# A two-layer hybrid backbone on one core: the third mixer's level scores with one product per level for both directions

## What is computed

```
def step(S, blk):
    qc, kc, vc, gc = blk
    b = jnp.cumsum(gc, axis=2)
    diff = b[:, :, :, None, :] - b[:, :, None, :, :]
    pair_decay = jnp.where(causal[:, :, None], jnp.exp(jnp.minimum(diff, 0.0)), 0.0)
    att = jnp.einsum('bhtd,bhsd,bhtsd->bhts', qc, kc, pair_decay)
    o = jnp.einsum('bhtd,bhdv->bhtv', qc * jnp.exp(b), S) + jnp.einsum('bhts,bhsv->bhtv', att, vc)
```

## Time and profile before

| | us |
|---|---|
| median of 3 runs | 1773.2 (1769.05 to 1775.02) |
| the profiled execution | 1773.12 |
| its span | 1771.1 |
| TensorE / weight load busy | 1602.1 / 1270.0 |
| VectorE / ScalarE / GpSimd busy | 1088.9 / 638.6 / 75.5 |
| mean DMA rate over the span | 103 GB/s, 182.01 MB |

### The profile page before, as it was taken

How to read it: one execution, slowest core, us unless ns; L and a number is a source line. 1 busy time by engine, 2 the same in 40 slices (tenths; PEclk the granted TensorE clock), 3 DMA queues, 4 the chain that set the end, 5 groups by cost and what they waited for, 6 DMA issues and landing times. The chain is left out here.

```text
span 1771.1 us, 29499 instructions
## 1 busy us (share of the span) xinstructions
PE 1602.1 (90%) x12128; PEld 1270.0 (72%) x12128; DVE 1088.9 (61%) x1868; ACT 638.6 (36%) x1062; POOL 75.5 (4%) x112
## 2 busy tenths in 40 slices
PE   6999999789789999999999979999968699889996
PEld 4766776655578778888887757678755587768875
DVE  2286347887866674554443354735788767668765
ACT  4254222433431254222222252433244321356651
POOL 0000011300101000000000000000020100000000
PEclk8999999989999999999999989989989899989999
DMA  9311111167201134222232022212234101345550
GB/s 391 140 48 49 55 53 60 57 242 260 76 3 50 41 127 167 95 95 95 96 118 72 1 87 83 73 48 83 73 118 146 50 2 50 119 191 186 181 204 24
DMA packets 41620, 182.01 MB, mean 103 GB/s; under 512 B 4752, under 2 KB 5520, under 8 KB 33680
## 3 DMA queue, kind: packets, MB, share of 16 engines
q1 hardware_dynamic: 41488, 180.14, 28.5%
HBM read 179.08 MB, written 1.05 MB: 102 GB/s over the span
## 5 line engine op out<-in xcount | busy, mean ns | idle before, releaser
L235 PE MATMUL ps<-hr_in,wr_in 128*128 128x512 f32 (+1 forms) x544 | 222.0, 408 | 14.2 <-DVE wr_in L228 13.1
L236 PE MATMUL ps<-hr_in,wr_in 128*128 128x512 f32 (+1 forms) x544 | 209.0, 384 | 0.0
L237 PE MATMUL ps<-hr_in,wr_in 128*128 128x512 f32 (+1 forms) x544 | 208.4, 383 | 0.0
L235 PEld LDWEIGHTS ps<-hr_in,wr_in 128*128 128x128 f32 x544 | 108.4, 199 | 63.7 <-issue 35.4
L228 DVE TENSOR_TENSOR wr_in<-mix,wr_in 128x1024 fp32r<-128x1024 f32 x68 | 83.9, 1235 | 95.5 <-ACT wr_in L224 91.5
L235 PE MATMUL ps<-mix_r,work_r 128*128 128x512 f32 (+1 forms) x352 | 133.8, 380 | 1.6 <-DVE work_r L228 1.6
L236 PE MATMUL ps<-work_r 128*128 128x512 f32 (+1 forms) x356 | 135.1, 379 | 0.0
L228 DVE TENSOR_TENSOR work_r<-pr,work_r 128x2048 fp32r<-128x2048 f32 x38 | 87.0, 2288 | 71.2 <-ACT work_r L224 67.0
L237 PE MATMUL ps<-mix_r,work_r 128*128 128x512 f32 x320 | 124.5, 389 | 0.0
L2970 PE MATMUL ps<-mix_r,work_r 128*128 128x512 f32 x336 | 121.4, 405 | 2.3 <-DVE mix_r L228 2.3
L237 PEld LDWEIGHTS ps<-hr_in,wr_in 128*128 128x128 f32 x544 | 108.2, 199 | 19.7
(11 more groups left out here) (522 smaller groups left out, 3314.2 us busy)
## 6 DMA issues: line engine op xcount, KB each, us to landing
mix<-in_w_in SPq DMA_DIRECT2D x68, 512.0 KB, 3.5
pr<-in_w_up SPq DMA_DIRECT2D x28, 1024.0 KB, 4.9
pr<-in_ada_w SPq DMA_DIRECT2D x40, 512.0 KB, 6.3
ring<-in_w_up SPq DMA_DIRECT2D x16, 1024.0 KB, 4.9
ring<-in_ada_w SPq DMA_DIRECT2D x28, 512.0 KB, 4.3
pr<-in_w_down SPq DMA_DIRECT2D x14, 1024.0 KB, 4.8
pr<-in_ada_w SPq DMA_DIRECT2D x8, 1024.0 KB, 15.7
work<-in_w_out SPq DMA_DIRECT2D x16, 512.0 KB, 3.6
```

The source lines that it names most:

```text
L235: nc.tensor.matmul(out, sh, mh, start=first, stop=False)
L236: nc.tensor.matmul(out, sh, ml, start=False, stop=False)
L237: return nc.tensor.matmul(out, sl, mh, start=False, stop=last)
```

## The change

Level scores of both directions come from one product. Of a block, the first half holds keys scaled for the forward direction and queries scaled for the backward one, the second half the reverse; the product's two off-diagonal quadrants are the forward and the backward scores. `steps` becomes (None, 0, 6, 1, 2, 3, 4, 5), eight entries. Step None is the diagonal: the keys of both directions are added, the queries taken unscaled, and collecting multiplies by the identity, which also writes the zeros that the GpSimd clear made before. The other levels are collected by a masked copy over all 128 columns into one image `at` of half the size. The widest level (number 2 of the steps, `WHOLE`) has no differences on VectorE: ScalarE makes its exponentials straight from the cumulated decay with a bias per partition, 64 columns at a time, and copies its quadrants out of PSUM itself (`collect_whole`). The keys' end decay is likewise made by ScalarE with a bias, 128 columns at a time. The read-out takes one image, so it has half the products. The extra work moves to other step numbers, and the jobs are dealt out over steps 1 to 7, so `late` holds five numbers in layer 0 and two in layer 1.

```diff
     vT = take(1024)
-    at = take(4096)
+    at = take(2048)
+    expo = (A1, take(2048))
     st = take(1024)
     A0 = take(3072)
-    expo = (A0[:, 0:1024], A1[:, 0:1024])
-    keys = (A0[:, 2048:3072], A1[:, 1024:2048])
+    keys = (A0[:, 0:1024], A0[:, 2048:3072])
...
-    steps = [(d, l) for l in range(LEVELS) for d in range(2)]
+    ecol, middle = tiles(mix, 0, 1)[:, 16:32], tiles(mix, 0, 1)[:, 32:48]
+    steps = (None, 0, LEVELS - 1, *range(1, LEVELS - 1))
+    WHOLE = 2
 
...
-    TURN_AT, PRODUCTS_AT, JOBS_AT = (3, 5), 7, 1
-    UNIT_AT = (11, 12)
-    KEYS_EXP_AT, QUERIES_EXP_AT, ENDS_EXP_AT, KEYS_OUT_AT = (1, 2), (4, 6), 3, (5, 7)
+    KEYS_AT, STATES_AT, QUERIES_AT = (2, 3), 6, (4, 5)
+    TURN_AT, PRODUCTS_AT, JOBS_AT = (3, 4), 5, 0
+    UNIT_AT = (6, 7)
+    KEYS_EXP_AT, QUERIES_EXP_AT, ENDS_EXP_AT, KEYS_OUT_AT = (1, 2), (3, 4), 3, (4, 5)
     use = len(steps) * len(pairs)
     ready = len(pairs) * (STATES_AT + 1)
...
                         pe.wait_ge(S("kv_out"), 1)
                     for b in range(4):
                         t0 = (b % 2) * T + jj[b // 2] * P
                         for q in range(2):
-                            mm = nc.tensor.matmul(score_bank(n, m, q)[:, b * P:(b + 1) * P], keys[d][q * HD:(q + 1) * HD, t0:t0 + P],
-                                                  queries[d][q * HD:(q + 1) * HD, t0:t0 + P], start=True, stop=True)
+                            mm = nc.tensor.matmul(score_bank(n, m, q)[:, b * P:(b + 1) * P], keys[n % 2][q * HD:(q + 1) * HD, t0:t0 + P],
+                                                  moving[q * HD:(q + 1) * HD, t0:t0 + P], start=True, stop=True)
                     mm.then_inc(S("s_mm"), 1)
                 if n in TURN_AT:
...
-                    for d in range(2):
-                        for q in range(2):
-                            hd = 2 * i + q
-                            mm = nc.tensor.matmul(ps[4 + i][q * HD:(q + 1) * HD, j * P:(j + 1) * P], vT[:, j * 256 + hd * HD:j * 256 + (hd + 1) * HD],
-                                                  at[:, d * 2048 + (4 * j + hd) * P:d * 2048 + (4 * j + hd + 1) * P],
-                                                  start=j == js[0] and d == 0, stop=False)
+                    for q in range(2):
+                        hd = 2 * i + q
+                        mm = nc.tensor.matmul(ps[4 + i][q * HD:(q + 1) * HD, j * P:(j + 1) * P], vT[:, j * 256 + hd * HD:j * 256 + (hd + 1) * HD],
+                                              at[:, (4 * j + hd) * P:(4 * j + hd + 1) * P], start=j == js[0], stop=False)
                 for j in js:
...
 
             pe.wait_ge(S("low_rank"), 1)
-            pe.wait_ge(S("at"), 2 * (idle_from + 1))
+            wait_collected(pe, idle_from)
             lora(0, 0)
             for p in late[:-2]:
...
@@ -1774,39 +1779,52 @@
 
             def exponents(n):
 
-                d, l = steps[n]
-                cv, dv = blocks(tiles(cum, 2 * d, 2), l), blocks(expo[d], l)
-                ref = (1 << l) - 1 if d == 0 else 1 << l
-                if n >= 2:
-                    dve.wait_ge(S("kf"), n - 1)
-                nc.vector.tensor_tensor(dv, cv, cv[:, :, :, ref:ref + 1].to_broadcast(list(cv.shape)),
-                                        ALU.subtract).then_inc(S("dv"), 1)
+                l = steps[n]
+                for d in range(2):
+                    cv, dv = blocks(tiles(cum, 2 * d, 2), l), blocks(tiles(expo[n % 2], 2 * d, 2), l)
+                    ref = (1 << l) - 1 if d == 0 else 1 << l
+                    if n == WHOLE:
+                        ins = nc.vector.tensor_scalar(middle_of(d).rearrange("p i (b t) -> p i b t", t=1), cv[:, :, :, ref:ref + 1], -1.0, None, ALU.mult)
+                    elif l == 0:
+                        ins = nc.vector.tensor_tensor(dv[:, :, :, 1 - d:2 - d], cv[:, :, :, 1 - d:2 - d], cv[:, :, :, d:d + 1], ALU.subtract)
+                    else:
+                        ins = nc.vector.tensor_tensor(dv, cv, cv[:, :, :, ref:ref + 1].to_broadcast(list(cv.shape)), ALU.subtract)
+                ins.then_inc(S("dv"), 1)
 
             def factors(n):
-                d, l = steps[n]
-                dve.wait_ge(S("exps"), n + 1)
-                if n >= 2:
-                    dve.wait_ge(S("s_mm"), len(pairs) * (n - 1))
-                nc.vector.tensor_tensor(later(queries[d], d, l), later(expo[d], d, l), later(tiles(pr, T_HQ, 2), d, l), ALU.mult)
-                nc.vector.tensor_tensor(sooner(keys[d], d, l), sooner(keys[d], d, l), sooner(tiles(pr, T_HF + 2 * d, 2), d, l),
-                                        ALU.mult).then_inc(S("kf"), 1)
+
+                l, k = steps[n], keys[n % 2]
+                if n == 0:
+                    nc.vector.tensor_tensor(two(k, layer), two(keys_of(0), layer), two(keys_of(1), layer), ALU.add).then_inc(S("kf"), 1)
+                    return
+                if l == 0:
+                    for d in range(2):
+                        nc.vector.tensor_copy(half(k, l, d == 1), half(keys_of(d), l, d == 1))
+                dve.wait_ge(S("exps"), n)
+                if l:
+                    for d in range(2):
+                        nc.vector.tensor_tensor(half(k, l, d == 1), half(k, l, d == 1), half(keys_of(d), l, d == 1), ALU.mult)
+                nc.vector.tensor_tensor(two(queries[n % 2], layer), two(queries[n % 2], layer), two(tiles(pr, T_HQ, 2), layer), ALU.mult)\
+                    .then_inc(S("kf"), 1)
 
             def collect(n):
-                d, l = steps[n]
-                B = 2 << l
+
+                l, done = steps[n], n - (n > WHOLE)
...
+                if n == WHOLE + 1:
+                    dve.wait_ge(S("at_whole"), 2 * len(pairs))
                 for m, jj in enumerate(pairs):
                     dve.wait_ge(S("s_mm"), len(pairs) * n + m + 1)
-                    o = d * 2048 + jj[0] * 512
                     for q in range(2):
-                        dst = at[:, o:o + 1024].rearrange("p (b q t) -> p b q t", b=4, q=2)[:, :, q, :]
+                        if n:
+                            dve.wait_ge(S("at"), 2 * len(pairs) * (done - 1) + 2 * m + q + 1)
+                        dst = at[:, jj[0] * 512:jj[0] * 512 + 1024].rearrange("p (b q t) -> p b q t", b=4, q=2)[:, :, q, :]
                         src = score_bank(n, m, q)[:, :].rearrange("p (b t) -> p b t", b=4)
-                        if l == 0:
-                            mask = c(C_BASE + d * P).bitcast(I32).rearrange("p (b t) -> p b t", b=1).to_broadcast([P, 4, P])
+                        mask = ident if n == 0 else c(C_BASE if l == 0 else C_LEVEL + l * P)
+                        if n == 0:
+                            ins = nc.vector.tensor_tensor(dst, src, mask.rearrange("p (b t) -> p b t", b=1).to_broadcast([P, 4, P]), ALU.mult)
                         else:
-                            part = slice(B // 2, B) if d == 0 else slice(0, B // 2)
-                            dst, src = (v.rearrange("p b (k t) -> p b k t", t=B)[:, :, :, part] for v in (dst, src))
-                            mask = halves(c(C_LEVEL + (d * LEVELS + l) * P).bitcast(I32), B, d == 0).to_broadcast(list(dst.shape))
-                        nc.vector.copy_predicated(dst, mask, src).then_inc(S("at"), 1)
...
-            exponents(0)
+            factors(0)
             exponents(1)
-            for n in range(len(steps)):
+            exponents(WHOLE)
+            for n in range(1, len(steps)):
                 factors(n)
-                if n + 2 < len(steps):
+                if n != WHOLE and n + 2 < len(steps):
                     exponents(n + 2)
+                for p in places(n)[:1] if n < len(steps) - 2 else ():
+                    spread_out(p)
+                if n - 1 != WHOLE:
+                    collect(n - 1)
                 if n == 1:
-                    dve.wait_ge(S("at0"), 1)
-                if n >= 1:
-                    collect(n - 1)
...
@@ -1859,7 +1875,7 @@
                 if n == UNIT_AT[1]:
                     nc.vector.tensor_tensor(norm, kk, kk, ALU.mult).then_inc(S("kk"), 1)
                 if n < len(steps) - 2:
-                    for p in places(n):
+                    for p in places(n)[1:]:
                         spread_out(p)
                 if n == len(steps) - 2:
...
+
+                l, k, q_ = steps[n], keys[n % 2], queries[n % 2]
+                act.wait_ge(S("dv"), n)
                 if n >= 2:
                     act.wait_ge(S("s_mm"), len(pairs) * (n - 1))
-                nc.scalar.activation(sooner(keys[d], d, l), sooner(expo[d], d, l), ACT.Exp, scale=-1.0).then_inc(S("k_exp"), 1)
-                if l == 0:
-                    act.wait_ge(S("k_exp"), n + 1)
-                nc.scalar.activation(later(expo[d], d, l), later(expo[d], d, l), ACT.Exp).then_inc(S("exps"), 1)
+                for d in range(2):
+                    sooner, later = d == 1, d == 0
+                    if n == WHOLE:
```

(57 more changed lines are left out.)

19 lines of the change are left out of this document (4 added, 15 removed).

## The result

The changed kernel took **1780.6 us** (median of 20 runs, 1774.5 to 1793.0) against 1772.6 (20 runs, 1765.9 to 1778.6) on the same chip: a ratio of 1.0053 [1.0035, 1.007], so 0.5% slower: 8.0 us between the medians, 9.4 by the ratio. The forecast was 1754 us, faster. The profiled execution has a span of 1778.1 us against 1771.1.

What follows compares the result with a forecast made beforehand. VectorE was taken as the busiest engine but for TensorE, with conditioning job loads also pacing layer 0. Layer 0's -7.5 and layer 1's -12.0 us sum to -19.5, from 1773.2 to 1754 us; range 1740 to 1765, rounded up by one.

Steps and rivals of the forecast that it cites:

- The terms of work: Third mixer: 14 to 8 score steps a layer; VectorE's level work 14.1 us less in layer 0, 8.4 in layer 1.
- All of it is covered by job 1: Layer 0's start: ScalarE's exponentials end by 362.7 us, hidden since TensorE is through with job 1 only at 367.
- Where it comes out, layer 0: Layer 0's loop and first read-out, laid out by hand: 7.5 us gained, between 0 and 14.
- scores of step 2 and job 2 373.7: Layer 0's early steps on TensorE: after job 1 at 367, these scores and job 2 are done at 373.7 us.
- From there a step is one chain: 11 to 13 us: Layer 0's steps after VectorE's release at 386 us: spreads, factors, differences, collecting, scores and turn or state products in sequence.
- job 8 ends at 430.4, job 9 at 438: Layer 0's end: the last two jobs come late, the first read-out behind them ends at 442.5 us against 448.2 before.
- Layer 1: Third mixer in layer 1: 8.4 us less VectorE work plus 3.9 less idle, less 0.3 for a spread product: -12.0 us.
- an idle time of 9.1 us in 14 steps leaves 5.2 in eight: Layer 1's loop: VectorE's idle time shrinks with the number of steps, giving 3.9 us.
- The first: Layer 0: VectorE decides and the jobs hide; -21 us there, total -33, 1740 us; chance 0.17.
- the second: Layer 0 gains nothing, paced by the job load cycle; -12 us in all, 1761 us; chance 0.20.
- The third: TensorE's clock falls in both layers, seven later steps at the lower level costing 10 and 6 us; 1770 us; chance 0.07.
- The fourth rival: Slower: in layer 0 exponentials behind ScalarE's row copies stop score steps under the loads; 1783 us; chance 0.06.

Runs made afterwards that it cites:

- experiment 4: Changed kernel, ScalarE copying job 0's row out ahead of the backward 64-column exponentials: 1778.6 us, ratio 1.0037 to the kernel before.
- Experiment 2: Changed kernel, VectorE's first spread addition moved behind the scores' collecting and the second into the next step, both layers: 1772.8 us, ratio 0.9988 to the kernel before.
- Experiment 5: Changed kernel, layer 0's last job and its spread products put behind the first read-out and low-rank products: 1775.1 us, ratio 1.001 to the kernel before.
- all3: Changed kernel with spread additions deferred, job 0's row copied early and job 9 behind the first read-out: 1761.8 us, ratio 0.9938 to the kernel before.
- experiment 1: Layer 0 runs the third mixer of the kernel before, layer 1 the changed one: 1765.8 us against 1774.6, ratio 0.9966.
- 6: Two kernels: changed kernel with spread additions deferred and job 9 behind the first read-out, without and with the early row copy: 1765.8 and 1761.8 us.
- experiment 8: Changed kernel, widest level given back to VectorE in both layers, without ScalarE's 64-column exponentials and quadrant copies: 1785.0 us, ratio 1.0071 to the kernel before.
- experiment 3: Changed kernel, only a step's first spread addition moved to the end of its own step, ahead of the second: 1778.1 us, ratio 1.0037 to the kernel before.

## Why the prediction was wrong

**The terms of work held.** Scores: 256 rows of TensorE in layer 0 and 128 in layer 1, the 384 forecast. VectorE: -15.0 and -9.0 us, forecast -14.1 and -8.4. ScalarE's 64-column exponentials list 0.33 us and start 0.24 apart, against 0.25 taken, by this row of the groups, 350.3 to 443 us, which answers to the earlier trace rows:

```profile
L1939 ACT ACTIVATE work<-hx 128x64 f32<-128x64 f32 x16 | 5.3, 333 | 1.1 <-PE ps L1673 1.1
```

The Trainium skill's figure (ScalarE: Activation LUTs, What ACT_TABLE_LOAD costs) gave 0.24, and this trace agrees. "All of it is covered by job 1" was too strong: TensorE waits 5.46 us for the row behind these exponentials, and job 1 is done at 372.1, 2.1 us later than laid out; experiment 4 shows that the load would have held TensorE for most of the wait anyway, and that some 1.5 us of it counted.

**The step that failed is "Where it comes out, layer 0"**: -7.5 us forecast, +10.7 measured (about +15 by the runs). I had named the very order that costs the time, and priced it wrongly, in three places. The laid-out times are moved by 3.0 us here, the later start of the stage.

- *"scores of step 2 and job 2 373.7"*: laid out 376.7, and job 2 ends at 384.8, 8.1 us late. 2.1 of them are job 1's. Then I set the scores directly behind job 1, as if their bank were free: collecting frees it, collecting stands behind the first spread addition, and TensorE waits 2.1 us. The products on the way ran at the lower level: 3.78 us for the scores, not 2.06, and twice 2.07 for a spread, not 1.1, together 3.7 us. With the next load and the scores of step 3 behind it, VectorE's release, laid out at 389, comes at 399.1: 10 us late in the first three steps.
- *"From there a step is one chain: 11 to 13 us"*: 12.5 and 15.1 measured (the factors at 399.06, 411.56 and 426.66), 3.6 us more. I summed rows at the upper level and booked every wait as if it cost the clock nothing. Three score steps in a row came at 3.8, 3.2 and 3.8 us.
- *"job 8 ends at 430.4, job 9 at 438"*, first read-out at 442.5: laid out 445.5, and 462.65 measured. Of these 17 us, 14 were there by job 9's end (455.1, laid out 441), those of the two places above, and 3 were lost in the tail, whose products I had counted at the upper level: 3.78 and 1.97 us for 1.9 and 1.0. "I take -7.5, between 0 and -14" then had no positive end at all, for a chain in which every product was taken at the upper level.

Experiment 2 acts on the first two and gains 11.0 us in the stage. Experiment 5 gains 10.6, and more than the 3 us that I had mis-sized at the end: it takes job 9 off the path of the first read-out, where the forecast had left it at 7.6 us (430.4 to 438). Together they give a stage of 108.9, 10.5 under the kernel before. So by the profiles the saving that I forecast for layer 0 was to be had, with another order. By the runs of both layers, `all3` is 11 us under the kernel before, of the 19.5 forecast.

**Layer 1**: -12.0 forecast, -7.7 by the profiles, -6 (2 to 10) by the runs. The term mis-sized is "an idle time of 9.1 us in 14 steps leaves 5.2 in eight". In the profile after, idle time did not shrink with the number of steps: over the stage it went from 11.3 to 12.6 us. In that of experiment 1, where layer 1's code is the same, it is 8.7 (63.8 - 55.1), so the size is not sure. A wait for a spread product stands there too, but behind another engine: VectorE waits 3.22 us for a product that itself waits 4.89 for ScalarE's copy of the row, which has quadrant copies (1.51 us) and exponentials (2.44 us) ahead of it. TensorE, then VectorE:

```profile
1344.36 2.07 PE L1642 MATMUL ps<-rowb,const 128*128 128x512 f32 x2 [4.89 <-ACT rowb L1969]
```

```profile
1346.47 0.69 DVE L1778 TENSOR_TENSOR gate<-gate,ps 128x512 f32<-128x512 f32 x1 [3.22 <-PE ps L1642]
```

Profiles of the changed layer 1 in kernels whose edits leave it alone lie between 63.8 and 72.4 us (75.5 in the kernel before), so its gain is known less well than its sign.

**The rivals.** The first (VectorE decides) and the second (layer 0 gains nothing) fall. The third, the clock, was right in direction (0.87 to 0.79 over the stage). It took seven score steps at the lower level, 10 us; seven list 21.0 us, 6.6 more than at 2.06 each. But it set this against a saving, and the waits had eaten that already. It was not only the score steps: TensorE as a whole lists 97.1 us for 98.3, where six steps fewer were to save 12.4. The clock of the stage was 0.80 in experiment 2, 0.83 in 5, and 0.88 and 0.86 in 6, so it came back as the stage lost its waits, little in the first. The rule of the Trainium skill cited there (TensorE: Matmul & The Clock Gate, Part 1: activity releases the clock) agrees in direction with this trace: 0.87 with TensorE idle for 21.2 us, 0.79 with 33.0. How much of the 10.7 us is idle time and how much is slower products on the path was not taken apart: keeping TensorE busy through the waits with products that nobody reads was not tried. The fourth rival had the sign and nearly the time (1783), by another mechanism: it blamed ScalarE's row copies and the exponentials ahead of them. Experiment 4 moved the copy for about 3 us by the runs, with intervals that overlap, and experiment 8 took the exponentials away, with more work on VectorE, to no gain.

**What stays open**: why the runs of kernels with the new layer 0 scatter more (1774 to 1793 after, 1757 to 1779 in experiment 2) than those of the kernel before (1766 to 1779); in experiment 3, the 4 us between profile and runs; and how the loss of layer 0 divides between waits and clock.

## What to carry to other kernels

When a loop gets fewer and shorter steps, side work dealt out over its steps gets denser: check for each engine in order that no side operation waits for a product of its own step, and that nothing which frees a bank stands behind one. Such an operation belongs one step later, after the freeing, and a side job that the next stage does not need belongs behind the result that it does need. And a chain laid out by hand from rows at the upper clock is a lower bound, not a middle: write a range for it that reaches to the rows at the lower one.

## What the runs showed of the hardware

- **Beside waits, the same products take longer.** Seven score steps of one shape took 21.0 us in the changed order and 16.8 in that of experiment 2; three of the long ones (granted 0.50, 0.74 and 0.50) follow a wait of 2.1 to 3.5 us for a bank, one a job that waited four times for its load.
- **Half the products, the same time.** 16 read-out products took 1.97 us at a granted clock of 0.50 and 1.09 at 1.00 (experiment 5); 32 took 1.97 at 1.00 in the kernel before.
- **A masked copy's price goes with its level.** In the kernel before, four copies of 256 columns took 2.45 us at level 1 (0.61 each), where the columns lie in runs of two, and 1.43 at level 2 (0.36), in runs of four, both with their operands ready. The later levels cost about what level 2 does. The mean of 0.49 that I used hides two prices:

```profile
371.11 2.45 DVE L1809 COPY_PREDICATED work<-const,ps 128x256 f32<-128x256 int32 x4
...
384.60 1.43 DVE L1809 COPY_PREDICATED work<-const,ps 128x256 f32<-128x256 int32 x4
```
